# Two transformer blocks in one program: rotary halves turned by DMA, and another order of gates, values and decays

## The reference

```python
z = x @ w_in
u, v, q, k, val, gates = jnp.split(z, SPLITS, axis=-1)
u = jax.nn.gelu(u); v = jax.nn.gelu(v)
h_a = _chunked_sgu(u, v, ...)        # u * (causal w_s @ layernorm(v) + b_s)
q = _rope(q, cos, sin); k = _rope(k, cos, sin)
o = _diff_attention(q, k, val, lam_full)
...
x1, x2 = jnp.split(xf, 2, axis=-1)   # in _rope
out = jnp.concatenate([x1 * c - x2 * s, x2 * c + x1 * s], axis=-1)
```

```python
z = einsum('bldr,drk->bldk', z_lr, w_alpha) + b_alpha
la = jnp.maximum(log_sigmoid(z) / GLA_GATE_TAU, GLA_LOG_ALPHA_MIN)
b = cumsum(la); q_dec = q * exp(b); k_inv = k * exp(-b); k_end = k * exp(b_last - b)
```

## Time and profile before

| | us |
|---|---|
| runs | 1823.33, 1823.72, 1816.3 |
| median | 1823.33 |
| the profiled execution | 1826.43 |
| its span | 1824.7 |
| granted clock over it | 0.996 |

### The profile page before, as it was taken

The page is one execution under the profiler, slowest core; times in us unless marked ns, Lnnn a source line. Parts: engine busy times, 40 slices in busy tenths (PEclk is TensorE's granted clock), DMA queues, the critical chain, the costliest instruction groups (busy, mean ns, idle before and its releaser), DMA issues.

```text
span 1824.7 us, 31051 instructions
## 1 busy us (share of the span) xinstructions
PE 1789.1 (98%) x12824; PEld 1618.3 (89%) x12824; DVE 1136.3 (62%) x1735; ACT 866.2 (47%) x1412; POOL 249.4 (14%) x264
## 2 busy tenths in 40 slices
PE   9999999999999999999999999999999899999998
PEld 8998699999899879997899997999787777889998
DVE  5764686686666466656675776566645555655553
ACT  5453344664445435443435753545345345445443
POOL 2000232121200020002321212000111343100000
PEclk9999999999999999999999999999999999999999
DMA  8565654446566666755745455675553333355553
GB/s 289 188 229 191 227 185 162 162 139 198 195 205 211 208 205 227 238 186 173 260 150 182 140 185 196 222 234 184 172 171 91 95 90 107 116 172 181 188 188 105
DMA packets 252397, 330.58 MB, mean 181 GB/s; under 512 B 13162, under 2 KB 213072, under 8 KB 252256
## 3 DMA queue, kind: packets, MB, share of 16 engines
q1 hardware_dynamic: 248240, 315.31, 53.0%
q0 software_dynamic: 4016, 13.27, 2.1%
HBM read 327.51 MB, written 1.05 MB: 180 GB/s over the span
## 4 chain that ended last, share of the span: by engine, by line
PE 62%; issue 24%; DVE 6%; POOL 3%; ACT 2%; DMA 2%; SPq 0%; POOLq 0%; DVEq 0%; ACTq 0%
PE bank L716 14%; PE bank L719 14%; PE bank L717 14%; PE bank L739 4%; PE bank L741 4%; PE bank L742 4%; DVE X L1939 1%; DMA G<-in_lam_dram 1%; DVE wlo L1861 1%; PE bank L1278 1%; ACT whi L1408 1%; POOL rs L2459 1%; PE bank L1256 1%; PE bank L904 1%; PE bank L942 1%
## 5 line engine op out<-in xcount | busy, mean ns | idle before, releaser
L1861 DVE TENSOR_TENSOR wlo<-raw,whi 128x1024 fp32r<-128x1024 f32 x537 | 664.2, 1241 | 383.6 <-ACT whi L1408 379.7
L1408 ACT ACTIVATE whi<-raw 128x1024 fp32r<-128x1024 f32 x549 | 574.2, 1051 | 390.5 <-PE bank L742 166.1
L716 PE MATMUL bank<-XTh,whi 128*128 128x256 f32 x1984 | 559.9, 282 | 0.0
L719 PE MATMUL bank<-XTh,wlo 128*128 128x256 f32 x1984 | 551.1, 278 | 0.0
L717 PE MATMUL bank<-XTl,whi 128*128 128x256 f32 x1984 | 550.8, 278 | 0.0
L716 PEld LDWEIGHTS bank<-XTh,whi 128*128 128x128 f32 x1984 | 373.4, 188 | 2.9
L717 PEld LDWEIGHTS bank<-XTl,whi 128*128 128x128 f32 x1984 | 374.0, 189 | 1.0
L719 PEld LDWEIGHTS bank<-XTh,wlo 128*128 128x128 f32 x1984 | 372.8, 188 | 0.4 <-DVE wlo L1861 0.3
L716 PE MATMUL bank<-HCh,whi 128*128 128x256 f32 (+1 forms) x880 | 252.4, 287 | 0.6 <-DVE tmp L2355 0.6
L717 PE MATMUL bank<-HCl,whi 128*128 128x256 f32 (+1 forms) x880 | 248.3, 282 | 0.0
L719 PE MATMUL bank<-HCh,wlo 128*128 128x256 f32 (+1 forms) x880 | 248.2, 282 | 0.0
(11 more groups left out here) (344 smaller groups left out, 2425.7 us busy)
## 6 DMA issues: line engine op xcount, KB each, us to landing
raw<-in_ffn_w_dram SPq DMA_DIRECT2D x131, 1024.0 KB, 5.1
raw<-in_w_in_dram SPq DMA_DIRECT2D x76, 1024.0 KB, 5.0
raw<-in_w_mod_dram SPq DMA_DIRECT2D x24, 1024.0 KB, 5.1
raw<-in_w_branch_dram SPq DMA_DIRECT2D x16, 1024.0 KB, 4.9
raw<-in_w_out_dram SPq DMA_DIRECT2D x12, 1024.0 KB, 4.8
raw<-in_w_ffn_gate_dram SPq DMA_DIRECT2D x11, 1024.0 KB, 5.2
raw<-in_w_ffn_up_dram SPq DMA_DIRECT2D x11, 1024.0 KB, 5.1
raw<-in_w_ffn_down_dram SPq DMA_DIRECT2D x8, 1024.0 KB, 5.2
```

Of the source, the lines that this page charges most:

```text
L716: e.matmul(o, hi[:, k, w0:w0 + nc_], xh, start=first and k == 0, stop=False)
L719: m = e.matmul(o, lo[:, k, w0:w0 + nc_], xh, start=False, stop=last and k == nk - 1)
L1408: e.activation(hi_part(n), raw_part(n), ACTF.Copy).then_inc(WHI.did(n), 1)
L1861: e.tensor_tensor(lo_part(n), raw_part(n), hi_part(n).bitcast(F32), ALU.subtract).then_inc(WLO.did(n), 1)
```

## The change

First block, in each mixer:

- The rotation matmuls and `perm` are gone. The half-swap of a tile is made by four DMAs of 32 partitions x 256 (32 KB each) from `mtmp` to another `mtmp` buffer: two issued by SP behind the load of a later chunk, two by POOL. New semaphores ROT and ROTP tell of their landing; the ring `mtmp` has eight buffers. DVE multiplies the turned tile by the sine, one tile later than before, and makes the sum too; POOL doesn't.
- `val` is computed ahead of u, with its chunks in the plan. V's statistics and norm on DVE move from ahead of q and k into `between_val`. The gating matmuls follow in four pieces u's products 1 to 4. ACT's high half and DVE's low half of the result lag by two tiles instead of one.
- A settle is added ahead of q and k and ahead of u, and at the end of every `mod_columns` (seven), where it carries the signal.

Second block: z is the first product behind vg, with the gates' matmuls behind qg0; ACT's g2 stands behind qg1; DVE's g2 is cut in four calls of one decay each, the first between the parts of q, the others behind the norms of the queries and about kg's parts; ACT's g3 ahead of the splits of k; POOL's decay products (QD, kw) ahead of its rotation of k.

```diff
@@ plan @@
+        first_qk.append(len(chunks))
         for c in range(2048, 4096, 256):
             chunk_a(w, 0, 8, c)
-        for c in range(0, 1024, 256):
-            chunk_a(w, 0, 8, c)
         for k in range(0, 8, 2):
             chunk_b(w, k, 2, 4096, 1024, MOVES)
+        for c in range(0, 1024, 256):
+            chunk_a(w, 0, 8, c)
...
+    chunk_a(w, 0, 8, 3072, 32)
     chunk_a(w, 0, 8, 1536)
     for k in (0, 4):
         chunk_b(w, k, 4, 0, 512, MOVES)
-    chunk_a(w, 0, 8, 3072, 32)
@@ sync @@
+            def turned(l, n):
+                ring_free(q, tm[l], ("u", n))
+                q.wait_ge(AMX, ("qk", l, n))
+                for p in (0, 32):
+                    e.dma_start(mtmp[tm[l].slot["u", n]][p:p + 32, :], mtmp[tm[l].slot["s", n]][p ^ 32:(p ^ 32) + 32, :]).then_inc(
+                        ROT[n % 4].did(("turned", l, n), by=16), 16)
...
             for c in range(1, before_bias):
                 load(c)
+                for l in range(2):
+                    if first_qk[l] <= c - 4 < first_qk[l] + 8:
+                        for j in range(2):
+                            turned(l, 2 * (c - 4 - first_qk[l]) + j)
@@ tensor @@
                 for j in range(4):
-                    mm = e.matmul(bank[b][:, 2 * j:2 * j + 2], spare[0:m, j * 128:(j + 1) * 128], cmb[0:m, :], start=True, stop=True)
-                mm.then_inc(MOD.did(("columns", g)), 1)
+                    e.matmul(bank[b][:, 2 * j:2 * j + 2], spare[0:m, j * 128:(j + 1) * 128], cmb[0:m, :], start=True, stop=True)
+                settle(b).then_inc(MOD.did(("columns", g)), 1)
...
+                empty(3)
+                settle(3)
                 for n in range(16):
                     gemm_a(bank[b][:, 0:T], xt, ("qk", l, n))
-                    if n:
-                        rotate(n - 1)
...
+                gemm_b(("val", l), 8, 1, xt_b, (0, 1), [[4, 5], [6, 7]], 1024, tail=2)
+                empty(3)
+                settle(3)
                 for n in range(8):
                     gemm_a(bank[b][:, 0:T], xt, ("u", l, n))
-                    if n == 0:
-                        rotate(15)
-                gemm_b(("val", l), 8, 1, xt_b, (0, 1), [[4, 5], [6, 7]], 1024, tail=2)
+                    if 1 <= n <= 4:
+                        spatial(n - 1)
@@ vector @@
                 for n in range(16):
                     w.pass_by(1)
+                    if n > 1:
+                        times_sin(n - 2)
                     if n:
-                        rotate(n - 1)
+                        times_cos(n - 1)
+                    if n > 1:
+                        add_parts(n - 2)
...
+                def between_q():
+                    n = slots.pop(0)
+                    if n < 2:
+                        rope("permq", n, QG[:, n, :], NT[ntr.slot["qg", n]], tmp[t2r.slot["uq", n]], B2["permq", n], 0.125)
+                    else:
+                        g2(0)
...
+                g2(1)
+                w.pass_by(1)
+                g2(2)
+                w.pass_by(1)
+                w.more(1)
+                g2(3)
@@ gpsimd @@
+                for n in range(16):
+                    w.pass_by(1)
+                    turned(n)
```

More of the change, by code:

```diff
@@ L278, in plan @@
     parts = [(c, j) for c in range(len(chunks)) for j in range(len(chunks[c][3]))]
-    return chunks, parts, whole, on_dve, before_bias
+    return chunks, parts, whole, on_dve, before_bias, first_qk
 MOVES, STANDS = 48, 0
@@ L317, in hold @@
         held.update(at[name] for name in names)
-    for n in range(2):
-        nb(("qg", n))
+    nb("z")
+    nb(("qg", 0))
+    for db in range(4):
+        nb(("gate", db))
+    nb(("qg", 1))
     hold([("q", t) for t in range(2)])
@@ L381, in program @@
     with ctx:
-        chunks, parts, whole, on_dve, before_bias = plan(I)
+        chunks, parts, whole, on_dve, before_bias, first_qk = plan(I)
         of_chunk = {}
@@ L395, in program @@
         BIAS = [signal(f"s_bias{h}") for h in range(8)]
+        ROT = [signal(f"s_rotary{i}") for i in range(4)]
+        ROTP = [signal(f"s_rotary_pool{i}") for i in range(4)]
         MM, TURN, SMALL, MOD = [signal("s_pe_" + n) for n in ("gemm", "turn", "small", "mod")]
@@ L912, in mixer, with spatial @@
                     emptied[b] = ((AMX, ("qk", l, n)),)
[L913 to L915 removed]
+                gemm_b(("val", l), 8, 1, xt_b, (0, 1), [[4, 5], [6, 7]], 1024, tail=2)
+                for b in range(4, 8):
+                    emptied[b] = ((AMX, ("val", l, (b - 4) // 2, b % 2)),)
+                empty(3)
+                settle(3)
+                def spatial(g2):
                     b = 6 + g2 % 2
@@ L1114, in g1 @@
                         emptied[b] = ((D2, ("min", db)),)
+                b = B2["z"]
+                empty(b)
+                gemm_a(bank[b][0:32, :], xj, "z", nc_=32)
+                emptied[b] = ((A2, "z"),)
+                for n in range(2):
+                    b = B2["qg", n]
+                    empty(b)
+                    gemm_a(bank[b][:, 0:T], xx, ("qg", n))
+                    emptied[b] = ((A2, ("qg", n)),)
+                    if n == 0:
+                        g1()
+                slots = [lambda: perm_g("permq", ("qg", 0), 0, B2["permq", 0]),
+                         lambda: perm_g("permq", ("qg", 1), 1, B2["permq", 1]), lambda: None]
+                gemm_b(("q",), 4, 2, xb, (0, 1), [[B2["q", t]] for t in range(2)], 512, tail=2, between=lambda: slots.pop(0)())
+                for t in range(2):
+                    emptied[B2["q", t]] = ((D2, ("turnq", t)),)
                 def g4():
@@ L1951, in mixer, with stats_v @@
                 w.more(3)
-                for t in range(2):
-                    if t:
-                        w.more(1)
+                def stats_v(t):
                     for c in range(2):
@@ L1982, in mixer, with spatial @@
+                w.more(3)
                 q.wait_ge(MIN[l], "in")
-                for g in range(8):
+                def spatial(g):
                     o = bank[6 + g // 2 % 2][:, (g % 2) * 256:(g % 2) * 256 + 256].rearrange("p (t c) -> p t c", t=2)
@@ L1994, in mixer @@
                     w.pass_by(1)
-                    if n == 0:
-                        rotate(15)
-                    else:
-                        low("ha", HAl, HAh, n - 1, mtmp[tm[l].slot["g", n - 1]])
-                low("ha", HAl, HAh, 7, mtmp[tm[l].slot["g", 7]])
-                w.pass_b(8, 2)
-                w.more(3)
+                    if 1 <= n <= 4:
+                        spatial(2 * n - 2)
+                        spatial(2 * n - 1)
+                    if n > 1:
+                        low("ha", HAl, HAh, n - 2, mtmp[tm[l].slot["g", n - 2]])
+                for n in (6, 7):
+                    low("ha", HAl, HAh, n, mtmp[tm[l].slot["g", n]])
                 for j in range(2):
@@ L2570, in second @@
                     e.tensor_tensor(LA[:, db, T:512], LA[:, db, T:512], KG[:, db % 2, T:512], ALU.mult).then_inc(P2.did(("kw", db)), 1)
+                for n in range(2):
+                    rotate("k", n, KG[:, n, 0:T])
                 w.pass_b(4, 2, tiles=4)
```

257 lines of the change are left out of this document (116 added, 141 removed).

## The result

| | before | after |
|---|---|---|
| runs, us | 1823.33, 1823.72, 1816.3, 1821.44 | 1798.22, 1800.13, 1805.25, 1801.32 |
| median, us | 1822.38 | 1800.72 |
| profiled execution, us | 1826.43 | 1798.22 |

The ratio is 0.989, with a 95% interval from 0.986 to 0.9921: 21.7 us less, of 14 to 26 that the interval allows. Forecast were 1796 us, between 1788 and 1811.

A forecast was written before the change was run, and what follows sets the result against it. TensorE, busy 98% of the span, was taken to bound the kernel. Mixers 17.8, settles 7.3 and second block 2.3 sum to 27.4 us, from the median 1823.3 to 1796 us, range 1788 to 1811.

The forecast's parts named there:

- The mixers: First block, both mixers: rotations leave TensorE, 101.2 us becomes 92.3, 8.9 per layer, 17.8 in all.
- The halves: Half-swap DMAs in q and k: TensorE loses zero, since products split ahead cover a lag of 3.6 us per layer.
- X = 6.5: DMA loop in q and k: halves landing up to 6.5 us after issue lose nothing; at 7.4 a chunk takes 5.9.
- The formula: Loop in q and k: chunk period is (landing time + 4.4 us of DVE work)/2, against TensorE's 5.45.
- Rival B: Mixers' q and k: halves land too late, over 1814 us; 6% in full, part loss within 16% shared with C, D.
- POOL's issues: Mixers' q and k: two DMA issues per product at 0.58 us, 1.2 of 2.71 us, hidden.
- Rival C: Mixers: POOL's issues stretch to 1.66 us each, 4.1 us lost per layer, 1804 us; within 16% for part losses.
- The settles: Seven settles behind mod_columns: the slow long runs become quick, 8.7 us gained, 1.4 us cost, net 7.3.
- rival A: Long matmul runs: the settle doesn't set the cadence, so 8.7 us is missing, 1805 us; chance 16%.
- The second block: Keys' wait of 5.53 us and 1.3 half clock go; queries' wait of 3.5 and 1.0 half clock come; gain 2.3.
- Rival D: Second block only moves its wait, the old one stays by half: gain there −3, 1801 us; within 16% for part losses.
- The lower end of −3: Second block's worst case: gain of −3 us if the old wait stays at half its length.

## Why the prediction was right, and where it wasn't

**The mixers, 17.8 forecast: 16.0 in the two traces, 15.4 in the kernel with that part alone.** No run has the rotations alone; what each part of the mixer gave is read from the traces. The rotations came off as reckoned; 0.44 per product went with each, q and k take 45.31 (slow) or 43.63 us (quick) with 43.6 reckoned. I had counted on the quick cadence for q and k and for u; q and k were quick in 3 of 16 cases, and u's last products in 1 of 26. That is the size missing. The other way, gating in four pieces costs 0.8 each, 3.2 in all, not 4.7, and the two settles 0.24, not 0.4. The sum on DVE costs 0.34, the lower end of its bounds, so DVE kept its half microsecond per product.

**The halves, zero forecast: zero, but for another reason than given.** No wait of PE in either mixer. I put the turning point at X = 6.5 and took 7.4 from the 96 KB row, with the lag that it brings covered. From SP's first issue to the last landing it was 5.7 to 7.6, 6.2 in the middle, so the lag was small. The formula left out the 0.6 to 1.0 us from the low part's end to that issue; with it the change lies where the formula turns. Its shape held where it was tried: with the loop over one chunk the same terms gave 10.4 us. Rival B was one load away, and came at once when that load was given.

**POOL's issues, hidden: yes.** 0.50 us each, 0.99 for two; 55 of the 64 had DVE at work beside them and took no longer than the other nine. Rival C is out. The Trainium skill's warning (SBUF — State Buffer, "SBUF: two separate sides") of 3.1 us concerns copies in a two-port mode; the 55 issues beside DVE's two-input operations show nothing of it, and it isn't contradicted, since no copy ran on DVE in that stretch.

**The settles, 7.3 forecast: nothing that can be told.** This is the step that failed. I took "six of six quick behind L776" as the work of L776; the trace has five such places, not six, and all five stand behind a layer norm's sums. That place kept the runs quick in 70 of 70 cases; what of it does so isn't shown, since two 2-column matmuls and a settle, put ahead of q and k to imitate it, left one layer quick and one slow. Behind other work the same transpose leaves the cadence open. The prediction's own sign for rival A, windows still slow behind a settle, came in both mixers. A's 1805 stood at 16%; the measured 1800.7 lies about midway between it and my 1796, so the time alone couldn't have told which of the two was right; the windows and the run with the settles alone did. I had also taken one profile's two slow runs for a property of the kernel, and so 8.7 us as there to be had, where the mean is 4.3. Nothing in a single trace could have told a chance from a property; the three times of before, 7 us apart, did hint at it, and the prediction says so but doesn't draw the conclusion.

**The second block, 2.3 forecast: 1.3 in the traces, nothing in the times.** The new wait was put at 3.5 and is 3.41; the old one went, 0.2 is left; the half clock behind the new wait was put at 1.0 and is 1.7. The mechanism of each step was right. Rival D did not come. The lower end of −3 was reckoned for less than it needs: the old wait at half its length alone leaves −1, and only with D's two low parts is it about −3.

**The sum.** 27.4 forecast, 21.7 measured. The mixers (16.0) and the second block (1.3) make 17.3; the 4.4 between this and the medians is inside what the interval leaves and isn't explained by a stage. So the time came out in the range with a term of 7.3 in it that no run shows: the mixers carried it, and the width of the range did the rest.

## What to carry to other kernels

A long run of one kind of matmul can have two cadences 4% apart, which fall anew in each execution, with odds that depend on what stands ahead: read it in several profiles before an edit is priced by it, and price the edit by the mean, not by the one profile in which it was slow. Where a load, a small DMA behind it and the engine that frees the load's buffer form a loop, count how many chunks the loop spans, from the freed buffer to the landing; one place in the queue, which took the loop from two chunks to one, made it 35 us per mixer here where it had cost nothing. And work that an engine does between two steps of a chain costs the main engine twice, by the wait and by the clock behind it: moving 2.9 us of DVE's work gave 4.0 us.

## What the runs showed that was not expected

The 256-column matmuls run at 113.3 or at 117.8 ns each, at full clock. A run settles on one or the other within its first eight matmuls at that clock and keeps it while nothing holds it up, for up to 1188 of them. Densely behind the layer norm's sums it was quick in 70 of 70 cases, behind the gating's matmuls slow in 25 of 26. What decides it stays open: it is not the program alone, since one program gave both.

The version with the first decay behind the query norms is quicker than both kernels: 1797.13 us beside 1802.21 for the changed one on the same chip, with 1799.0 the slowest of its executions and 1799.9 the quickest of the other's.
